# A feed-forward's convolution over tokens, done on transposed gates, is done instead on gates with tokens on the partitions

## The chip, the cores and the metric

The kernel runs on one core of a Trainium2 chip, which has eight. The metric is the time of one execution on the device, in microseconds (us). TensorE multiplies matrices, VectorE (DVE) and ScalarE (ACT) work on elements, GpSimd (POOL) does a small part, and SyncE (SP) and ScalarE issue the transfers, which run on the core's DMA engines. SBUF is the memory on the chip, with 128 partitions; PSUM takes TensorE's results.

## The reference

Two transformer blocks run one after the other on x of 256 tokens by 2048 channels, all in float32. The change touches the end of the second block, the feed-forward with a short causal convolution over the tokens on its gate:

```
h = rms_norm_2(x, ffn_norm_g[i])
val, gate = jnp.split(h @ w_up[i], 2, axis=-1)          # 2048 -> 2 x 5632
gate = causal_depthwise_conv(gate, conv_w[i], conv_b[i])
x = x + (val * jax.nn.gelu(gate, approximate=False)) @ w_down[i]

def causal_depthwise_conv(x, w, b):                     # w: 3 x 5632
    xp = jnp.pad(x, ((0, 0), (2, 0), (0, 0)))
    y = b
    for k in range(3):
        y = y + w[k] * xp[:, k:k + l]
    return y
```

Token s of a gate channel thus needs tokens s-1 and s-2 of the same channel. The first block's feed-forward has SiLU in place of convolution and GELU: silu(h @ w_gate) * (h @ w_up), then the down projection.

## The kernel before

**Panels and pieces.** Every matrix product is cut into panels of 512 output columns. The tokens are two tiles of 128 (t = 0, 1), so a panel has two accumulators in PSUM (`ACC`, four banks in all, two panels in turn). The rows of a weight panel come in chunks of 4 x 128 rows, one transfer of 1 MB each, in four slots; a chunk is two pieces. A piece of the wide panels is 2 x 128 rows of weights, and costs TensorE 12 products: for each tile and each 128 rows `weights_hi*xT_hi`, `weights_lo*xT_hi`, `weights_hi*xT_lo` (lines 602 to 604 in `panel`). A wide panel has 8 pieces.

**The split.** Float32 weights are cut in two before use. For each piece ScalarE writes the high part (`weights_hi`, line 1233) and VectorE the rest (`weights_lo`, line 1811). Both do it three pieces ahead of TensorE, in a ring of four: ScalarE's split of piece g+3 waits until TensorE has finished piece g-1, and TensorE waits for `lo_split` of a piece before its first product.

**Side work.** Everything else hangs in generators. After each piece every engine's program calls `side.step()`, which runs its next stretch of side work up to a `yield`; so a number of yields places side work in a panel. The engines' programs are written apart and meet by semaphores only. The order on each engine is thus fixed, and one that waits in a side step holds up its own next split.

**The second feed-forward** has 11 pairs of panels, gate then value ("up"). ScalarE evacuates the gate's accumulators to `ffn_gate` (`FF1`, line 1385) when the gate panel is multiplied, VectorE the value's to `ffn_hidden` (`FF2`, line 1971). Both have tokens on the partitions. `ffn_turn` then runs in the next gate panel's steps: TensorE transposes gates and values (line 626, product with an identity), 16 blocks of 128 x 128 for a pair, all after the second piece. With channels on the partitions the convolution is a shift along the row: VectorE computes it from PSUM (`conv2`, lines 2009 and 2015; its weights are one number for each partition), ScalarE does GELU (line 1404), VectorE multiplies with the value (line 2027), and the product is split into `hiddenT_hi` (ScalarE, line 1406) and `hiddenT_lo` (VectorE, line 2031), in two halves `kp`. After the last pair the turning has no spread: it comes after the first piece of the down projection.

**The first feed-forward** evacuates with SiLU (line 1385), multiplies in the evacuation of the value (line 1974), and so turns only products: 8 transposes for each pair, then one copy and one subtraction for each half (lines 1409 and 1992).

The convolution's weights come at the start as rows (`vectors`), are turned by TensorE, and lie in `V2`.

Of the kernel before, what the change touches and what calls it, by code (L numbers as in the profile page):

```python
# [14 lines left out]
P = 128  # L15
# [28 lines left out]
PIECES = 4  # L44
PAIRS = 8
# [45 lines left out]
class Events:  # L91
# [8 lines left out]
        mixed ffn_turned hidden_hi hidden_lo convolved gelu_ready gated_ready rows_applied  # L100
# [8 lines left out]
    LOADS = """x_load0 x_load1 x_load2 x_load3 x_load4 second_piece fourth_piece rows0 rows1 rows2 rows3 rows4 decay gla_b norm_rows dt b_proj c_proj v_bias sinks  # L109
        gate_rows0 gate_rows1 glu_rows stores""".split()  # L110
# [11 lines left out]
class Memory:  # L122
# [10 lines left out]
    def on_chip(self):  # L133
# [20 lines left out]
        self.V2 = small("vectors2", [P, 4 * KF])  # L154
# [55 lines left out]
        self.CG = sb("conv_gelu", [P, 2, S], R + 96 * K)  # L210
# [55 lines left out]
        self.ROWS = [sb(f"rows{i}", [P, P], 90 * K + R + 512 * i) for i in range(5)]  # L266
# [226 lines left out]
class Tensor:  # L493
# [8 lines left out]
    def program(self):  # L502
# [50 lines left out]
        self.ffn(plan.ffn1, side, False)  # L553
# [29 lines left out]
        self.ffn(plan.ffn2, side, True)  # L583
# [125 lines left out]
    def ffn(self, panels, side, second):  # L709
        m = self.m  # L710
        X = (m.XH, m.XL)
        for i, (gate, up) in enumerate(panels):
            if i:
                side.add(self.ffn_turn(panels[i - 1], second, spread=True))
# [3 lines left out]
        side.add(self.ffn_turn(panels[-1], second, spread=False))  # L718

    def ffn_turn(self, pair, second, spread):  # L720
# [3 lines left out]
        for kp in range(2):  # L724
# [399 lines left out]
class Scalar:  # L1124
# [161 lines left out]
    def load_rows4(self):  # L1286
        act, t, rows, ev = self.act, self.t, self.m.ROWS[4], self.ev
        vec = lambda x: x.rearrange("(k p) -> k p", p=P)
        at = 0
        for n in ("norm2_w", "attn_norm_g_2", "ffn_norm_g_2"):  # L1290
            act.dma_start(rows[at:at + KD, :], vec(t[n][0])).then_inc(ev["loaded_rows4"], 16)
            at += KD
        act.dma_start(rows[at:at + 2, :], vec(t["gla_norm_w"][0])).then_inc(ev["loaded_rows4"], 16)
        act.dma_start(rows[at + 2:at + 26, :],
                      t["conv_w"][0].rearrange("j (k p) -> (j k) p", p=P)).then_inc(ev["loaded_rows4"], 16)
# [6 lines left out]
    def vectors(self):  # L1302
        act, t, m, ev = self.act, self.t, self.m, self.ev
        vec = lambda x: x.rearrange("(k p) -> k p", p=P)
        cw = t["conv_w_2"][0].rearrange("j (k p) -> (j k) p", p=P)
        for i, at, n, src in ((1, 0, 88, cw[0:88, :]), (2, 0, 44, cw[88:132, :]), (2, 44, 44, vec(t["conv_b_2"][0])),
                              (3, 0, 14, vec(t["b_in_2"][0, 0:QKVU2])), (3, 14, 4, vec(t["ssm_d_2"][0])),
# [1173 lines left out]
```

## Time and profile before

| | |
|---|---|
| time, median of 3 runs | 2893.9 us (2893.78 to 2893.98) |
| the profiled execution's own time | 2893.83 us |
| its span in the profile | 2892.6 us |
| TensorE busy | 2879.3 us (100%) |
| VectorE / ScalarE busy | 1634.0 us (56%) / 1321.1 us (46%) |
| granted TensorE clock | 1.00 of full speed, 2.4 GHz, nearly throughout |

The busy share is that of the span. Matmuls overlap, so the busy time of TensorE shows that it seldom stood without work, and not how fast it went; the distance between the starts of two instructions shows what one of them costs.

### The profile page before, as it was taken

What the parts mean: (1) busy time and instruction counts of PE and PEld (TensorE: products, weight loads), DVE (VectorE), ACT (ScalarE), POOL (GpSimd) and SP (SyncE); (2) the same over time, 40 slices, a digit from 0 to 9 for tenths busy, and PEclk for the clock granted to TensorE, in tenths of its full rate; (3) what the DMA queues carried; (4) which work ended last, traced back from release to release, by engine and by line L of the source; (5) the groups of instructions that cost most, each with busy time, mean ns of one, the idle gap of its engine ahead of it and who ended that gap; (6) DMA issues with size and microseconds to landing.
All of it is one profiled execution on the core that took longest, in us unless ns stands there. A gap on an engine that the chain in (4) does not pass through costs nothing.

```text
span 2892.6 us, 32563 instructions
## 1 busy us (share of the span) xinstructions
PE 2879.3 (100%) x13522; PEld 2380.4 (82%) x13522; DVE 1634.0 (56%) x1874; ACT 1321.1 (46%) x1627; POOL 183.1 (6%) x221
## 2 busy tenths in 40 slices
PE   9999999999999999999999999999999999999998
PEld 8878887788888888888888888887888888888887
DVE  5464555555555554554475457655755665656444
ACT  5444445444444444444454455444554444444443
POOL 0000000000000000000000029900100000000000
PEclk9999999999999999999999999999999999999999
DMA  7555454555555555555665556554655555555563
GB/s 257 198 166 195 155 188 149 174 190 189 196 187 184 188 190 190 189 190 189 205 193 182 185 175 198 171 171 153 206 187 189 189 178 189 183 192 192 186 204 131
DMA packets 279392, 536.86 MB, mean 186 GB/s; under 512 B 17361, under 2 KB 20365, under 8 KB 279245
## 3 DMA queue, kind: packets, MB, share of 16 engines
q1 hardware_dynamic: 267520, 528.52, 55.8%
q10 hardware_dynamic: 11725, 6.27, 0.8%
q8 instruction: 107, 1.75, 0.2%
q14 instruction: 40, 0.33, 0.0%
HBM read 532.65 MB, written 2.10 MB: 185 GB/s over the span
## 4 chain that ended last, share of the span: by engine, by line
PE 99%; DVE 0%; ACT 0%; issue 0%; POOL 0%; POOLq 0%; ACTq 0%
PE panels L602 31%; PE panels L604 31%; PE panels L603 31%; PE side L626 3%; DVE weights_lo L1811 0%; PE side L919 0%; PE side L615 0%; PE side L996 0%; PE side L915 0%; PE side L904 0%; PE side L783 0%; PE side L1089 0%; PE side L1088 0%; PE side L1065 0%; PE side L800 0%; PE side L817 0%
## 5 line engine op out<-in xcount | busy, mean ns | idle before, releaser
L1811 DVE TENSOR_TENSOR weights_lo<-weights,weights_hi 128x1024 fp32r<-128x1024 f32 (+1 forms) x1032 | 1254.6, 1220 | 1077.5 <-ACT weights_hi L1233 1074.8
L1233 ACT ACTIVATE weights_hi<-weights 128x1024 fp32r<-128x1024 f32 (+1 forms) x1032 | 1066.3, 1036 | 1218.0 <-PE panels L604 1198.4
L602 PE MATMUL panels<-weights_hi,xT_hi 128*128 128x512 f32 (+1 forms) x2748 | 1077.4, 392 | 0.1
L604 PE MATMUL panels<-weights_hi,xT_lo 128*128 128x512 f32 (+1 forms) x2752 | 1069.3, 389 | 0.0
L603 PE MATMUL panels<-weights_lo,xT_hi 128*128 128x512 f32 (+1 forms) x2752 | 1068.7, 388 | 0.0
L602 PEld LDWEIGHTS panels<-weights_hi,xT_hi 128*128 128x128 f32 x2748 | 516.4, 188 | 111.1 <-issue 7.3
L604 PEld LDWEIGHTS panels<-weights_hi,xT_lo 128*128 128x128 f32 x2752 | 517.0, 188 | 107.3
L603 PEld LDWEIGHTS panels<-weights_lo,xT_hi 128*128 128x128 f32 x2752 | 517.5, 188 | 103.2 <-issue 0.2
L602 PE MATMUL panels<-weights_hi,hiddenT_hi 128*128 128x512 f32 x704 | 275.2, 391 | 0.0
L604 PE MATMUL panels<-weights_hi,hiddenT_lo 128*128 128x512 f32 x704 | 274.2, 390 | 0.0
L603 PE MATMUL panels<-weights_lo,hiddenT_hi 128*128 128x512 f32 x704 | 274.2, 389 | 0.0
L604 PEld LDWEIGHTS panels<-weights_hi,hiddenT_lo 128*128 128x128 f32 x704 | 132.2, 188 | 27.5
L602 PEld LDWEIGHTS panels<-weights_hi,hiddenT_hi 128*128 128x128 f32 x704 | 132.2, 188 | 27.2
L603 PEld LDWEIGHTS panels<-weights_lo,hiddenT_hi 128*128 128x128 f32 x704 | 132.3, 188 | 26.9
L402 POOL TENSOR_TENSOR rstd<-mean_squares,minus_half 128x2 f32<-128x2 f32 x5 | 4.4, 876 | 1270.4 <-DVE mean_squares L1874 1270.4
L602 PE MATMUL panels<-weights_hi,merged2T_hi 128*128 128x512 f32 x128 | 50.4, 394 | 0.3 <-issue 0.3
L602 PE MATMUL panels<-weights_hi,mixedT_hi 128*128 128x512 f32 x128 | 50.2, 392 | 0.0
L604 PE MATMUL panels<-weights_hi,merged2T_lo 128*128 128x512 f32 x128 | 49.9, 390 | 0.0
L604 PE MATMUL panels<-weights_hi,mixedT_lo 128*128 128x512 f32 x128 | 49.9, 390 | 0.0
L603 PE MATMUL panels<-weights_lo,merged2T_hi 128*128 128x512 f32 x128 | 49.9, 390 | 0.0
L603 PE MATMUL panels<-weights_lo,mixedT_hi 128*128 128x512 f32 x128 | 49.8, 389 | 0.0
L402 POOL TENSOR_TENSOR rstd_first<-mean_squares,minus_half 128x2 f32<-128x2 f32 x1 | 0.7, 688 | 737.9 <-DVE mean_squares L1874 737.9
(356 smaller groups left out, 1914.6 us busy)
## 6 DMA issues: line engine op xcount, KB each, us to landing
weights<-in_w_in SPq DMA_DIRECT2D x162, 1024.0 KB, 5.0
weights<-in_w_up SPq DMA_DIRECT2D x88, 1024.0 KB, 5.1
weights<-in_w_ffn_gate SPq DMA_DIRECT2D x44, 1024.0 KB, 5.2
weights<-in_w_ffn_up SPq DMA_DIRECT2D x44, 1024.0 KB, 5.2
weights<-in_w_out SPq DMA_DIRECT2D x32, 1024.0 KB, 5.1
weights<-in_w_ffn_down SPq DMA_DIRECT2D x32, 1024.0 KB, 5.1
weights<-in_w_down SPq DMA_DIRECT2D x32, 1024.0 KB, 5.1
weights<-in_w_ffn_down SPq DMA_DIRECT2D x16, 768.0 KB, 4.5
```

The source lines that it names most:

```text
L402: self.pool.tensor_tensor(dst[:, 0:2], self.m.MS[:, 0:2], self.m.NHALF[:, 0:2], ALU.pow).then_inc(self.ev["rstd_ready"])
L602: pe.matmul(acc, a, wh, start=k0 + k == 0, stop=False)
L603: pe.matmul(acc, a, wl, start=False, stop=False)
L604: inst = pe.matmul(acc, b, wh, start=False, stop=k0 + k == total - 1)
L626: return self.pe.transpose(out, in_, self.m.IDENT[0:in_.shape[0], 0:in_.shape[0]])
L1233: self.act.activation(self.m.HI[:, g % PIECES, 0:n], raw, ACT.Copy).then_inc(self.ev["hi_split"])
L1811: self.dve.tensor_tensor(m.LO[:, ring, 0:n], raw, m.HI[:, ring, 0:n].bitcast(F32), ALU.subtract).then_inc(self.ev["lo_split"])
```

## The change

The second feed-forward's convolution moves to where the gates have tokens on their partitions. The shift by one or two tokens is then a shift of partitions, and DMA makes it: after ScalarE has evacuated a gate panel, it issues six transfers from `ffn_gate` to two new tiles `gate_shifted1` and `gate_shifted2` (`shift_gates`): for each shift one of 112 partitions, one of 15 or 14, and one of 1 or 2 that takes the end of tile 0 to the start of tile 1. The weights and the bias are now needed as rows that are the same in all partitions: four transfers of 256 KB for each pair (`conv_rows`), issued by ScalarE behind the pair's GELU for the next pair.

VectorE's convolution (`conv2`) is six operations of 128 x 1024, two after each other for each shift, in steps 5 to 8 of the value panel; ScalarE's GELU is one operation of 128 x 1024 in its step 8. The value's evacuation multiplies by it at once, as in the first feed-forward, but waits for `gelu_ready`. TensorE then turns only the product, so both feed-forwards share `ffn_turn`. The convolution's weights no longer pass through `vectors`: three transfers, two transposes and two copies there are gone, and so is `V2`.

```diff
--- before.py
+++ after.py
...
-        self.CG = sb("conv_gelu", [P, 2, S], R + 96 * K)
+        self.GS1 = sb("gate_shifted1", [P, TT, PANEL], R + 96 * K)
+        self.GS2 = sb("gate_shifted2", [P, TT, PANEL], 80 * K + 512)
+        self.WR1 = sb("conv_rows01", [P, 2, PANEL], R + 40 * K)
+        self.WR2 = sb("conv_rows2b", [P, 2, PANEL], R + 84 * K)
...
-        for i, n, loads in ((1, 88, 1), (2, 88, 2), (3, 50, 4), (4, 74, 5)):
+        for i, n, loads in ((1, 50, 4), (2, 74, 5)):
...
-            if second:
-                b0, b1 = self.bank(2 * kp), self.bank(2 * kp + 1)
-                for k in range(2):
-                    for t in range(TT):
-                        f = (2 * kp + k) * P
-                        o = slice(k * S + t * P, k * S + (t + 1) * P)
-                        self.tr(b0[:, o], m.FF1[:, t, f:f + P])
-                        inst = self.tr(b1[:, o], m.FF2[:, t, f:f + P])
-                self.free(2 * kp, "gated_ready", n - 2 * (FF // PANEL))
-                self.free(2 * kp + 1, "gated_ready", n - 2 * (FF // PANEL))
-            else:
-                inst = self.four(self.bank(kp), lambda k, t: m.FF2[:, t, k * P:(k + 1) * P], 2 * kp)
-                self.free(kp, "hidden_lo", n)
-            inst.then_inc(ev["ffn_turned"])
-        for _ in range((5 if second else 4) if spread else (4 if second else 2)):
+            self.four(self.bank(kp), lambda k, t: m.FF2[:, t, k * P:(k + 1) * P], 2 * kp).then_inc(ev["ffn_turned"])
+            self.free(kp, "hidden_lo", n)
+        for _ in range(4 if spread else 2):
             yield
         if not spread:
-            for _ in range(5 if second else 0):
-                yield
             pe.wait_ge(ev["hidden_lo"], self.ffn_turns)
...
+        if second:
+            side.add(self.conv_rows(panels[0][0], self.plan.out2[-1].end))
...
-            if i and second:
-                act.wait_ge(ev["ffn_turned"], n0 + 2 * i)
...
+            if second:
+                side.finish()
+                self.shift_gates(gate)
+                side.add(self.gelu(i, panels))
             self.panel(up, side)
             side.finish()
-        side.add(self.ffn_turn(len(panels) - 1, second, spread=False, rows=rows, pair=panels[-1]))
-
-    def ffn_turn(self, i, second, spread, rows=None, pair=None):
+        side.add(self.ffn_turn(len(panels) - 1, spread=False, rows=rows, pair=panels[-1]))
+
+    def conv_rows(self, gate, end):
+        act, m, ev, t = self.act, self.m, self.ev, self.t
+        act.wait_ge(ev["multiplied"], end)
+        cols = slice(gate.col - FF, gate.col - FF + PANEL)
+        for dst, src in ((m.WR1[:, 0, :], t["conv_w_2"][0][0, cols]), (m.WR1[:, 1, :], t["conv_w_2"][0][1, cols]),
+                         (m.WR2[:, 0, :], t["conv_w_2"][0][2, cols]), (m.WR2[:, 1, :], t["conv_b_2"][0][cols])):
+            act.dma_start(dst, src.partition_broadcast(P)).then_inc(ev["loaded_conv_rows"], 16)
+        yield
+
+    def shift_gates(self, gate):
+        act, m, ev = self.act, self.m, self.ev
+        self.wait_evacuated(gate)
+        for s, dst in ((1, m.GS1), (2, m.GS2)):
+            act.dma_start(dst[s:MAIN + s, :, :], m.FF1[0:MAIN, :, :]).then_inc(ev["loaded_shifted"], 16)
+            act.dma_start(dst[MAIN + s:P, :, :], m.FF1[MAIN:P - s, :, :]).then_inc(ev["loaded_shifted"], 16)
+            act.dma_start(dst[0:s, 1, :], m.FF1[P - s:P, 0, :]).then_inc(ev["loaded_shifted"], 16)
+
+    def gelu(self, i, panels):
+        act, m, ev = self.act, self.m, self.ev
+        for _ in range(7):
+            yield
+        act.wait_ge(ev["convolved"], i + 1)
+        act.activation(m.FF1[:, :, :], m.FF1[:, :, :], ACT.Gelu).then_inc(ev["gelu_ready"])
+        if i + 1 < len(panels):
+            yield from self.conv_rows(panels[i + 1][0], panels[i][0].end)
...
-            if second:
-                yield
-                k = n - 2 * (FF // PANEL)
-                act.wait_ge(ev["convolved"], k)
-                act.activation(m.CG[:, :, :], m.CG[:, :, :], ACT.Gelu).then_inc(ev["gelu_ready"])
-                act.wait_ge(ev["gated_ready"], k)
-                act.activation(hh, m.CG[:, :, :], ACT.Copy).then_inc(ev["hidden_hi"])
-            else:
-                act.wait_ge(ev["ffn_turned"], n)
-                act.activation(hh, m.SIDE[:, kp, :], ACT.Copy).then_inc(ev["hidden_hi"])
+            act.wait_ge(ev["ffn_turned"], n)
+            act.activation(hh, m.SIDE[:, kp, :], ACT.Copy).then_inc(ev["hidden_hi"])
             yield
             if spread and kp == 0:
                 yield
-                if not second:
-                    yield
+                yield
...
+        if second:
+            dve.memset(m.GS1[0:1, 0, :], 0.0)
+            dve.memset(m.GS2[0:2, 0, :], 0.0)
         for i, (gate, up) in enumerate(panels):
             if i:
-                side.add(self.ffn_turn(i - 1, second, spread=True))
+                side.add(self.ffn_turn(i - 1, spread=True))
             self.panel(gate, side)
+            if second:
+                side.finish()
+                side.add(self.conv2(i))
             self.panel(up, side)
             side.finish()
             dve.wait_ge(ev["multiplied"], up.end)
             if i:
                 dve.wait_ge(ev["ffn_turned"], n0 + 2 * i)
             for t in range(TT):
-                acc, r = m.ACC[:, (up.index % 2) * TT + t, :], m.RSTD[:, t:t + 1]
                 if second:
-                    dve.tensor_scalar(m.FF2[:, t, :], acc, r, None, ALU.mult).then_inc(up.evac[t][0])
+                    dve.wait_ge(ev["gelu_ready"], i + 1)
                 else:
                     dve.wait_ge(*gate.evac[t])
-                    dve.scalar_tensor_tensor(out=m.FF2[:, t, :], in0=acc, scalar=r, in1=m.FF1[:, t, :],
-                                             op0=ALU.mult, op1=ALU.mult).then_inc(up.evac[t][0])
-        side.add(self.ffn_turn(len(panels) - 1, second, spread=False))
-
-    def ffn_turn(self, i, second, spread):
+                dve.scalar_tensor_tensor(out=m.FF2[:, t, :], in0=m.ACC[:, (up.index % 2) * TT + t, :],
+                                         scalar=m.RSTD[:, t:t + 1], in1=m.FF1[:, t, :], op0=ALU.mult,
+                                         op1=ALU.mult).then_inc(up.evac[t][0])
+        side.add(self.ffn_turn(len(panels) - 1, spread=False))
...
+    def conv2(self, i):
+        dve, m, ev, step = self.dve, self.m, self.ev, self.step
+        w0, w1, w2, bias = (r[:, j, :].unsqueeze(1).to_broadcast([P, TT, PANEL]) for r in (m.WR1, m.WR2) for j in range(2))
+        g = m.FF1[:, :, :]
+        for _ in range(4):
+            yield
+        dve.wait_ge(ev["loaded_shifted"], 16 * 6 * (i + 1))
+        dve.wait_ge(ev["loaded_conv_rows"], 16 * 4 * (i + 1))
+        step(dve.tensor_tensor(g, g, w2, ALU.mult))
+        for shifted, w in ((m.GS1, w1), (m.GS2, w0)):
+            yield
+            step(dve.tensor_tensor(shifted[:, :, :], shifted[:, :, :], w, ALU.mult))
+            step(dve.tensor_tensor(g, g, shifted[:, :, :], ALU.add))
+        yield
+        dve.tensor_tensor(g, g, bias, ALU.add).then_inc(ev["convolved"])
+        yield
```

On TensorE this is the row of the second feed-forward where the first pair is turned, before and after (`side` is the PSUM tile that takes transposes).

```order
L603 MATMUL panels<-weights_lo,xT_hi 128x512
L604 MATMUL panels<-weights_hi,xT_lo 128x512
L626 MATMUL side<-identity,ffn_gate 128x128
L626 MATMUL side<-identity,ffn_hidden 128x128
L626 MATMUL side<-identity,ffn_gate 128x128
L626 MATMUL side<-identity,ffn_hidden 128x128
L626 MATMUL side<-identity,ffn_gate 128x128
L626 MATMUL side<-identity,ffn_hidden 128x128
```

```order
L606 MATMUL panels<-weights_lo,xT_hi 128x512
L607 MATMUL panels<-weights_hi,xT_lo 128x512
L629 MATMUL side<-identity,ffn_hidden 128x128 x8
L605 MATMUL panels<-weights_hi,xT_hi 128x512
L606 MATMUL panels<-weights_lo,xT_hi 128x512
L607 MATMUL panels<-weights_hi,xT_lo 128x512
L605 MATMUL panels<-weights_hi,xT_hi 128x512
```

Of the sixteen transposes for each pair, the eight of the gates are gone (the first block shows half of the sixteen); their place behind the second piece is the same.

On VectorE, from the evacuation of the first value panel on. Before:

```order
L2031 TENSOR_TENSOR hiddenT_lo<-conv_gelu,hiddenT_hi 128x512
L1811 TENSOR_TENSOR weights_lo<-weights,weights_hi 128x1024 x10
L1971 TENSOR_SCALAR ffn_hidden<-panels,rstd 128x512 x2
L1811 TENSOR_TENSOR weights_lo<-weights,weights_hi 128x1024 x2
L2009 TENSOR_SCALAR conv_gelu<-side,vectors_59 128x256 x2
L2015 SCALAR_TENSOR_TENSOR conv_gelu<-side,vectors_59,conv_gelu 128x255 x2
L2015 SCALAR_TENSOR_TENSOR conv_gelu<-side,vectors_59,conv_gelu 128x254 x2
L1811 TENSOR_TENSOR weights_lo<-weights,weights_hi 128x1024
L2027 TENSOR_TENSOR conv_gelu<-side,conv_gelu 128x512
L2031 TENSOR_TENSOR hiddenT_lo<-conv_gelu,hiddenT_hi 128x512
L1811 TENSOR_TENSOR weights_lo<-weights,weights_hi 128x1024 x2
L2009 TENSOR_SCALAR conv_gelu<-side,vectors_59 128x256 x2
```

After, from the last splits of the second value panel (`conv_rows01`, `conv_rows2b` are weights and bias, `gate_shifted1` and `2` the shifted gates; the number behind a name tells copies apart):

```order
L1817 TENSOR_TENSOR weights_lo<-weights,weights_hi 128x1024 x8
L2014 TENSOR_TENSOR ffn_gate<-ffn_gate,conv_rows2b 128x1024
L1817 TENSOR_TENSOR weights_lo<-weights,weights_hi 128x1024
L2017 TENSOR_TENSOR gate_shifted_108<-gate_shifted_108,conv_rows_110 128x1024
L2018 TENSOR_TENSOR ffn_gate<-ffn_gate,gate_shifted_108 128x1024
L1817 TENSOR_TENSOR weights_lo<-weights,weights_hi 128x1024
L2017 TENSOR_TENSOR gate_shifted_109<-gate_shifted_109,conv_rows_110 128x1024
L2018 TENSOR_TENSOR ffn_gate<-ffn_gate,gate_shifted_109 128x1024
L1817 TENSOR_TENSOR weights_lo<-weights,weights_hi 128x1024
L2020 TENSOR_TENSOR ffn_gate<-ffn_gate,conv_rows2b 128x1024
L1985 SCALAR_TENSOR_TENSOR ffn_hidden<-panels,rstd,ffn_gate 128x512 x2
L1817 TENSOR_TENSOR weights_lo<-weights,weights_hi 128x1024 x2
```

The convolution went from the gate panel that follows, between two and three splits behind the evacuation, to the last four splits of the value panel itself, ahead of the evacuation.

On ScalarE, before, from the second gate panel's end, and after, the same place:

```order
L1385 ACTIVATE ffn_gate<-panels,rstd 128x512 x2
L1233 ACTIVATE weights_hi<-weights 128x1024 x11
L1404 ACTIVATE conv_gelu<-conv_gelu 128x512
L1406 ACTIVATE hiddenT_hi<-conv_gelu 128x512
L1233 ACTIVATE weights_hi<-weights 128x1024 x3
L1404 ACTIVATE conv_gelu<-conv_gelu 128x512
L1406 ACTIVATE hiddenT_hi<-conv_gelu 128x512
L1233 ACTIVATE weights_hi<-weights 128x1024 x2
```

```order
L1370 ACTIVATE ffn_gate<-panels,rstd 128x512 x2
L1393 DMA gate_shifted_108<-ffn_gate 112x1024
L1394 DMA gate_shifted_108<-ffn_gate 15x1024
L1395 DMA gate_shifted_108<-ffn_gate 1x16x32
L1393 DMA gate_shifted_109<-ffn_gate 112x1024
L1394 DMA gate_shifted_109<-ffn_gate 14x1024
L1395 DMA gate_shifted_109<-ffn_gate 2x512
L1222 ACTIVATE weights_hi<-weights 128x1024 x8
L1402 ACTIVATE ffn_gate<-ffn_gate 128x1024
L1386 DMA conv_rows_110<-in_conv_w 128x512 x2
L1386 DMA conv_rows2b<-in_conv_w 128x512
L1386 DMA conv_rows2b<-in_conv_b 128x512
```

The six shifting transfers stand ahead of the split that follows the evacuation; GELU and four more transfers stand ahead of the split of the next gate panel's fourth piece.

## Rows read from the trace of the kernel before

**Rows 1.** The page: span, busy time and share of each engine, times instructions.

```profile
span 2892.6 us, 32563 instructions
...
PE 2879.3 (100%) x13522; PEld 2380.4 (82%) x13522; DVE 1634.0 (56%) x1874; ACT 1321.1 (46%) x1627; POOL 183.1 (6%) x221
```

**Rows 2.** The page: the chain that ended last, shares by engine.

```profile
PE 99%; DVE 0%; ACT 0%; issue 0%; POOL 0%; POOLq 0%; ACTq 0%
```

**Rows 3.** ScalarE's timeline: gate evacuations of both feed-forwards (start, duration, instruction).

```profile
1008.55 1.27 ACT L1385 ACTIVATE ffn_gate<-panels,rstd 128x512 f32<-128x512 f32 x2 [1.60 <-PE panels L604]
...
1052.99 1.27 ACT L1385 ACTIVATE ffn_gate<-panels,rstd 128x512 f32<-128x512 f32 x2 [1.60 <-PE panels L604]
...
2166.03 1.27 ACT L1385 ACTIVATE ffn_gate<-panels,rstd 128x512 f32<-128x512 f32 x2 [1.60 <-PE panels L604]
...
2211.34 1.27 ACT L1385 ACTIVATE ffn_gate<-panels,rstd 128x512 f32<-128x512 f32 x2 [1.54 <-PE panels L604]
```

**Rows 4.** TensorE's timeline, a block of sixteen transposes, second feed-forward.

```profile
2192.80 0.40 PE L604 MATMUL panels<-weights_hi,xT_lo 128*128 128x512 f32 x1
2193.03 0.27 PE L626 MATMUL side<-identity,ffn_gate 128*128 128x128 f32 x1
2193.14 0.27 PE L626 MATMUL side<-identity,ffn_hidden 128*128 128x128 f32 x1
...
2195.01 0.39 PE L603 MATMUL panels<-weights_lo,xT_hi 128*128 128x512 f32 x1
```

**Rows 5.** TensorE's weight loads, the same place.

```profile
2192.80 0.14 PEld L626 LDWEIGHTS side<-identity,ffn_gate 128*128 128x128 f32 x1
```

**Rows 6.** TensorE's timeline, the four vector transposes near the start.

```profile
47.38 0.72 PE L626 MATMUL side<-identity,rows 88*128 88x88 f32 x4
...
48.22 0.39 PE L603 MATMUL panels<-weights_lo,xT_hi 128*128 128x512 f32 x1
```

**Rows 7.** VectorE's timeline in the second feed-forward.

```profile
2187.78 1.41 DVE L1971 TENSOR_SCALAR ffn_hidden<-panels,rstd 128x512 f32<-128x512 f32 x2 [0.34 <-PE panels L604]
...
2194.11 1.00 DVE L2009 TENSOR_SCALAR conv_gelu<-side,vectors 128x256 f32<-128x256 f32 x2 [1.23 <-PE side L626]
2195.14 1.78 DVE L2015 SCALAR_TENSOR_TENSOR conv_gelu<-side,vectors,conv_gelu 128x255 f32<-128x255 f32 x4
2196.83 1.22 DVE L1811 TENSOR_TENSOR weights_lo<-weights,weights_hi 128x1024 fp32r<-128x1024 f32 x1
...
2223.32 1.23 DVE L1811 TENSOR_TENSOR weights_lo<-weights,weights_hi 128x1024 fp32r<-128x1024 f32 x1 [1.43 <-ACT weights_hi L1233]
2226.10 1.23 DVE L1811 TENSOR_TENSOR weights_lo<-weights,weights_hi 128x1024 fp32r<-128x1024 f32 x1 [1.55 <-ACT weights_hi L1233]
```

**Rows 8.** ScalarE by line and shape, 2140 to 2650 us: count, busy, mean.

```profile
L1233 ACT ACTIVATE weights_hi<-weights 128x1024 fp32r<-128x1024 f32 x180 | 189.5, 1058 | 199.5 <-PE panels L604 197.2 <-POOL rstd L402 2.3
...
L1404 ACT ACTIVATE conv_gelu<-conv_gelu 128x512 f32<-128x512 f32 x21 | 13.3, 633 | 40.3 <-DVE conv_gelu L2015 40.3
```

**Rows 9.** Tile gate_bias_rows: issue duration (min/median/max ns) and microseconds to landing.

```profile
L1685 ACTq DMA_DIRECT2D gate_bias_rows<-in_b_in x8: 334/334/353, 1761.2 to 1939.2; - x8
...
DMA to landing us min/median/max: 3.0/4.7/6.3
```

**Rows 10.** Tile rows: the longest issue on ScalarE's queue.

```profile
L1291 ACTq DMA_DIRECT2D rows<-in_norm_w x1: 607/607/607, 37.7 to 37.7; - x1
```

**Rows 11.** Transfers: size of each, median microseconds to landing.

```profile
weights<-in_w_up SPq DMA_DIRECT2D x88, 1024.0 KB, 5.1
...
norm_rows<-in_final_norm_g ACTq DMA_DIRECT2D x1, 1024.0 KB, 4.9
...
w_a_down<-in_w_in ACTq DMA_DIRECT2D x1, 128.0 KB, 17.1
```

**Rows 12.** Busy time of each engine by stretch, at the end, with granted clock (PEclk).

```profile
core 0: us, PE busy (x) PEld busy (x) DVE busy (x) ACT busy (x) POOL busy (x), PEclk, DMA share, GB/s
...
2880.00:2884.00 4.00, 1.94 (x9) 1.28 (x7) 2.63 (x4) 1.32 (x4) 0.00 (x0) 1.00 0.00 0
2884.00:2888.00 4.00, 0.00 (x0) 0.00 (x0) 2.31 (x7) 1.89 (x4) 0.69 (x1) 0.63 0.33 125
```

More of the change, by code:

```diff
@@ L265, in on_chip @@
         self.FF2 = sb("ffn_hidden", [P, TT, PANEL], R + 92 * K)
-        self.ROWS = [sb(f"rows{i}", [P, P], 90 * K + R + 512 * i) for i in range(5)]
+        self.ROWS = [sb(f"rows{i}", [P, P], 90 * K + R + 512 * i) for i in range(3)]
 class Plan:
@@ L552, in program @@
         self.residual(plan.out1, (m.MH, m.ML), side, rows=False, turn=True)
-        self.ffn(plan.ffn1, side, False)
+        self.ffn(plan.ffn1, side)
         side.add(self.ssm_setup())
@@ L707, in residual, with ffn @@
             side.add(self.norm_panel(p, pan, rows, turn))
-    def ffn(self, panels, side, second):
+    def ffn(self, panels, side):
         m = self.m
@@ L713, in ffn @@
             if i:
-                side.add(self.ffn_turn(panels[i - 1], second, spread=True))
+                side.add(self.ffn_turn(panels[i - 1], spread=True))
             self.panel(gate, X, side)
@@ L717, in ffn, with ffn_turn @@
             side.finish()
-        side.add(self.ffn_turn(panels[-1], second, spread=False))
-    def ffn_turn(self, pair, second, spread):
+        side.add(self.ffn_turn(panels[-1], spread=False))
+    def ffn_turn(self, pair, spread):
         pe, ev, m = self.pe, self.ev, self.m
@@ L1284, in turn, with load_rows2 @@
             yield
-    def load_rows4(self):
-        act, t, rows, ev = self.act, self.t, self.m.ROWS[4], self.ev
+    def load_rows2(self):
+        act, t, rows, ev = self.act, self.t, self.m.ROWS[2], self.ev
         vec = lambda x: x.rearrange("(k p) -> k p", p=P)
@@ L1867, in vectors @@
             yield
-        for i in (1, 2, 3, 4):
+        for i in (1, 2):
             self.dve.wait_ge(self.ev["vectors"], i + 1)
@@ L1958, in ffn @@
         n0 = 2 * len(panels) if second else 0
+        if second:
+            dve.memset(m.GS1[0:1, 0, :], 0.0)
+            dve.memset(m.GS2[0:2, 0, :], 0.0)
         for i, (gate, up) in enumerate(panels):
             if i:
-                side.add(self.ffn_turn(i - 1, second, spread=True))
+                side.add(self.ffn_turn(i - 1, spread=True))
             self.panel(gate, side)
+            if second:
+                side.finish()
+                side.add(self.conv2(i))
             self.panel(up, side)
@@ L1984, in ffn_turn @@
             self.ffn_turns += 1
[L1985 to L1993 removed]
+            k = slice(at + 2 * kp, at + 2 * kp + 2)
+            self.dve.wait_ge(self.ev["hidden_hi"], self.ffn_turns)
+            self.dve.tensor_tensor(m.HL[:, k, :], m.SIDE[:, kp, :], m.HH[:, k, :].bitcast(F32),
+                                   ALU.subtract).then_inc(self.ev["hidden_lo"])
             yield
@@ L1996, in ffn_turn @@
                 yield
-                if not second:
-                    yield
-    def conv2(self, at, kp):
-        dve, m, ev, n = self.dve, self.m, self.ev, self.ffn_turns
-        G, b0 = m.CG, m.SIDE[:, 2 * kp, :]
-        vec = lambda j, k: m.V2[:, at + (j * KF + 2 * kp + k):at + (j * KF + 2 * kp + k) + 1]
-        dve.wait_ge(ev["ffn_turned"], n)
-        if n > 1:
-            dve.wait_ge(ev["hidden_hi"], n - 1)
-            dve.wait_ge(ev["hidden_lo"], n - 1)
-        for k in range(2):
-            self.mark(dve.tensor_scalar(G[:, k, :], b0[:, k * S:(k + 1) * S], vec(2, k), vec(3, k),
-                                        ALU.mult, ALU.add))
-        for j in (1, 0):
-            s = 2 - j
-            self.settle()
-            for k in range(2):
-                inst = dve.scalar_tensor_tensor(
-                    out=G[:, k, s:S], in0=b0[:, k * S:(k + 1) * S - s], scalar=vec(j, k), in1=G[:, k, s:S],
-                    op0=ALU.mult, op1=ALU.add)
-                if j:
-                    self.mark(inst)
-        inst.then_inc(ev["convolved"])
```

53 lines of the change are left out of this document (16 added, 37 removed).

## Prediction

> **What bounds the kernel now.** I read the page first: TensorE is busy for 2879.3 of the span's 2892.6 us [rows 1], and 99% of the chain that ended last are its instructions [rows 2]. So there is hardly a wait to remove. An edit pays if it takes instructions from TensorE's row, and costs where TensorE must wait for something new. What VectorE and ScalarE do is free until TensorE waits for it. Next I read ScalarE's evacuations of the gates, which mark the pairs: the pairs of the first feed-forward lie 1052.99 - 1008.55 = 44.44 us apart, those of the second 2211.34 - 2166.03 = 45.31 us [rows 3]. Both have the same 192 products; they differ by 8 transposes. The other pairs repeat these distances within 0.03 us.
>
> **What TensorE saves.** The difference, 45.31 - 44.44 = 0.87 us, is the price of the 8 gate transposes of a pair, 0.109 us each. The block itself agrees: from the product at 2192.80 to the one at 2195.01 are 2.21 us, of which two product distances of 0.227 (44.44 us less 0.87 for the first feed-forward's own 8 transposes, by 192) are no transposes, so (2.21 - 0.45) / 16 = 0.110 [rows 4]. Eleven pairs: 11 x 0.87 = **-9.6 us**. Near the start four vector transposes take 48.22 - 47.38 - 0.23 = 0.61 us [rows 6]; two of them go: **-0.3 us**. The transfers and copies that go with them lie on ScalarE beside a busy TensorE: nothing.
>
> **What ScalarE gets.** I count from the start of a gate's evacuation, 2211.34 [rows 3], as zero. A piece lasts 2.72 us: the value panel's eight end at 2187.78 - 2166.03 = 21.75 [rows 3, 7]. The evacuation ends at 1.27. It is awaited (hand-overs take 0.03: VectorE's two operations from 2194.11 end at 2195.11, the dependent one starts at 2195.14 [rows 7]), and then come six transfers to issue. The trace shows no issue of a copy from SBUF to SBUF. The nearest row is 0.334 us each for 128 rows [rows 9], the longest 0.607 [rows 10]: together 2.0 to 3.6. Then the split, 1.06 [rows 8], and VectorE's, 1.23 [rows 7]: done at 5.7 to 7.3. Behind the waiting split stands TensorE's fourth piece. Its weight load would start at 3 x 2.72 less 0.42 = 7.74, since a load stands about 0.42 ahead of the moment at which the others see the piece before as done (2192.80 [rows 5] against 2187.78 + 5.44 [rows 7]). It is in time at both ends: nothing. The four broadcast transfers behind GELU are 1.3 us of issue by 0.334 and precede a split that TensorE wants at 21.75 + 7.74 = 29.5; ScalarE is free for it by 27. Nothing.
>
> **Do the shifts land in time?** The first multiplication comes at 13.1 (below). The issues end by 1.3 + 3.6 = 4.9 at the latest, which leaves 8.2 us. Both shifts are 896 KB. The rows for transfers from HBM beside the same weight stream: 256 KB 3.0 to 6.3 us [rows 9], 1 MB 4.9 us, a weight chunk 5.1 [rows 11]. I take 5 to 6.5: in time. The other end is 17.1 us for a transfer of short runs in the crowded start [rows 11]. I keep it for a rival, as these runs are long. The weight chunks themselves are issued some 19 us (seven pieces) before their first split and need 5.1, so they have room for 2 MB more for each pair.
>
> **When VectorE lets the products go.** This is the step that decides. The convolution stands in the value panel's steps 5 to 8, each behind a split. The split of step 5 starts at 2223.32 - 2211.34 = 11.98, that of step 6 at 2226.10 - 2211.34 = 14.76 [rows 7]. Back to back the next operation starts 0.09 before the one ahead ends (the run from 2195.14 ends at 2196.92, the next starts at 2196.83 [rows 7]), so a split of 1.23 costs 1.14. The six operations of 128 x 1024 have the shape of the split; I take its 1.22, and 1.25 where the next must wait for the result. First multiplication: 13.12 to 14.34, before the next split. Then from 14.76 without a pause: split 1.14, two operations 2.50, split 1.14, two operations 2.50, split 1.14, bias 1.22. Convolved at 24.40. GELU on ScalarE: 128 x 1024 takes 1.06 in the split; GELU at 512 costs 0.633, of which a second 512 would add about the same 0.43 [rows 8]. 24.43 + 1.06 = 25.49. The evacuation with the product: two operations, 1.41 [rows 7], so 25.52 + 1.41 = 26.93, and TensorE sees it at 26.96.
>
> TensorE wants it after two pieces of the next gate panel: the first transpose's load started at 2192.80, 5.02 behind the panel's end [rows 5, 7], that is at 21.75 + 5.02 = 26.77. It is late by 0.19. Of this, 0.12 costs nothing, because a transpose's product normally starts 0.23 behind its load (2193.03 [rows 4, 5]) and needs only the 0.11 of a transpose's distance. That leaves 0.07; I take 0.1, for ten pairs **+1.0 us**.
>
> The eleventh pair has no such room: it is turned after one piece of the down projection, so wanted at 26.77 - 2.72 = 24.05. Late by 2.91, less 0.12: **+2.8 us**. Before, the value was free at 21.75 + 1.41 and nothing waited. Nothing else is late next: while TensorE stands, both splits catch up, and `hidden_lo` of this pair follows in time: from the transposes at 27.2, ScalarE has two copies of 0.63 and two splits of 1.06 [rows 8], to 30.6, then VectorE's subtraction of some 0.7, to 31.3. TensorE wants it after two more pieces, at 33.
>
> Bounds. If the six operations were as slow as two evacuations of 512 (1.41), the five behind 14.76 would add 0.95: 1.0 a pair more, and 2899. If they took only ScalarE's 1.06, nothing waits in the ten pairs and the last waits 2.0: 2886.0.
>
> **Sum.** -9.6 - 0.3 + 1.0 + 2.8 = -6.1 us against the profiled execution's own 2893.83: 2887.7. The median of the runs is 0.07 above it, so 2887.8 us. A measurement of this kernel tells about 0.2% (5.8 us) from no change; the line is at 2888.1, so the forecast lies on it.
>
> **A rule and a row.** TensorE's last work ends 1.94 us behind 2880, at 2881.94. The granted clock is 1.00 (2.4 GHz) over 2880 to 2884 and averages 0.63 over 2884 to 2888 [rows 12]; if it fell in one step to half (1.2 GHz), then at about 2885.0, 3.1 us after the last work. The wait at the last pair is 2.8 us. The Trainium skill, "TensorE: Matmul & The Clock Gate", section "Part 1: The HAM clock gate", says that activity holds the clock up and an idle TensorE falls to half rate; the trace agrees with the fall. By the rule the stall may cost more than its length; by the sum it costs its length alone.
>
> **The rivals.**
> *No wait in the ten pairs.* Speaks for it that 0.07 is less than the error of a sum of ten durations. Then 2886.8. Chance 0.12.
> *A larger wait.* A broadcast operand, or a longer hand-over than 0.03 at each of five places, puts 0.3 to 1.0 on each pair: 2890 to 2898. Against it: no row shows a 1024 operation in SBUF slower than 1.22 here, while GpSimd is idle. Chance 0.18.
> *The clock falls at the last pair.* For it the rows above, against it that 2.8 is under what passed there. Each us at half speed costs 0.5 more; for 2 to 8 us, 2889 to 2892. Chance 0.07.
> *The shifts land late* (the other side). Each us beyond 13.1 delays the whole chain by one in all eleven pairs. It decides from 1.1 us late on: 6.1 + 5.8 = 11.9 us by 11. With the 17.1 of [rows 11] for the last transfer: 4.9 + 17.1 - 13.1 = 8.9 late, 98 us, near 2986. Against it are all rows of long transfers. Chance 0.08.
> *The gates still pass TensorE*: excluded by the order of rows above.
> The forecast itself, waits of 0 to 0.2 a pair, 2886.8 to 2889, has 0.5, two thirds of it below the line; 0.05 is for what I don't see.
>
> **How the numbers follow.** Faster: 0.33 + 0.12 = 0.45. Slower: 0.08 and half of what I don't see, 0.11. The rest, 0.44, is within 0.2%. The range leaves out the upper part of the larger wait and the late landing, and reaches below to all operations at 1.06: 2886.0 to 2895.0.
>
> **What would show it.** Right: pairs of the second feed-forward 44.44 to 44.6 apart; GELU starting 24.4 behind the gate's evacuation; eight transposes of products only; a wait of 2.8 us of TensorE ahead of the last transposes, for the value's evacuation. Wrong: VectorE's first multiplication idle for a DMA; splits waited for by TensorE; pairs above 45; a clock under 1.00 near 2640.

## The result and the profile after

The changed kernel takes 2898.52 us (median; 2896.94 to 2899.77 in 20 runs), the kernel before in the same comparison 2893.82 us (2893.35 to 2894.09). The ratio is 1.0016, 95% interval 1.001 to 1.0023: 4.7 us slower, where 2887.8 was forecast and 2895.0 was the end of the range. By the bound of 0.2% that is no change, but the interval leaves out equality, and the forecast gain of 6 us is not there. The runs also spread over 2.8 us, against 0.7 before.

The page of the changed kernel's profiled run (2898.11 us) shows where to look. These are its span, TensorE's part of the busy line, the queue that carries the shifts, and the chain.

```profile
span 2896.8 us, 32398 instructions
PE 2875.9 (99%) x13432; PEld 2367.3 (82%) x13432; DVE 1634.1 (56%) x1788; ACT 1313.8 (45%) x1614; POOL 183.6 (6%) x221
q10 hardware_dynamic: 21702, 29.18, 3.3%
PE 95%; ACTq 2%; DVE 1%; ACT 1%; issue 0%; DMA 0%; SPq 0%; POOL 0%; DVEq 0%
```

Against [rows 1] TensorE has 90 instructions and 3.4 us of busy time less (99% of the span where it was 100%). The span is 4.2 us longer. Against [rows 2] the chain has lost 4% to others, the largest of them ACTq: instructions that issue transfers on ScalarE. DMA has 0% of it (rounded), so hardly anything on the path waited for bytes. The waits between 2150 and 2700 us say who waits for whom (us in total, times, longest). In the kernel before none of TensorE's rows stands in this list.

```profile
ACT ffn_gate L1402 <- DVE ffn_gate L2020: 46.7, 11, 4.4
DVE ffn_hidden L1985 <- ACT ffn_gate L1402: 13.4, 11, 1.2
PEld side L629 <- issue: 9.5, 11, 3.3
PEld panels L605 <- DVE weights_lo L1817: 6.9, 11, 0.9
PE side L629 <- DVE ffn_hidden L1985: 5.1, 11, 2.9
PE panels L605 <- DVE weights_lo L1817: 2.1, 10, 0.5
```

Two waits have come, each eleven times. One is for VectorE's split of a weight piece (L1817), the other, ahead of the transposes (L629), for the evacuation with the product (L1985). A wait's length is not its cost: a weight load normally runs ahead of its product, so what is lost is read from the distances of the products.

**The first wait, on ScalarE.** ScalarE's timeline at the pair of [rows 3], with its issues (ACTq), up to the next pair:

```profile
2210.87 1.27 ACT L1370 ACTIVATE ffn_gate<-panels,rstd 128x512 f32<-128x512 f32 x2 [1.60 <-PE panels L607]
2212.22 0.59 ACTq L1393 DMA_DIRECT2D gate_shifted<-ffn_gate  x1
2212.85 0.86 ACTq L1394 DMA_DIRECT2D gate_shifted<-ffn_gate  x1
2213.74 0.87 ACTq L1395 DMA_DIRECT2D gate_shifted<-ffn_gate  x1
2214.64 0.61 ACTq L1393 DMA_DIRECT2D gate_shifted<-ffn_gate  x1
2215.28 0.81 ACTq L1394 DMA_DIRECT2D gate_shifted<-ffn_gate  x1
2216.11 0.65 ACTq L1395 DMA_DIRECT2D gate_shifted<-ffn_gate  x1
2216.81 3.90 ACT L1222 ACTIVATE weights_hi<-weights 128x1024 fp32r<-128x1024 f32 x4 [4.67 <-PE panels L607]
...
2235.88 1.06 ACT L1402 ACTIVATE ffn_gate<-ffn_gate 128x1024 f32<-128x1024 f32 x1 [4.37 <-DVE ffn_gate L2020]
...
2256.20 1.27 ACT L1370 ACTIVATE ffn_gate<-panels,rstd 128x512 f32<-128x512 f32 x2 [1.60 <-PE panels L607]
```

The six issues take 4.39 us of their own, 4.54 from the first's start to the last's end, where the forecast allowed 2.0 to 3.6. The split behind them starts at 2216.81. The bracket names TensorE as its releaser, but that product had long been done (the idle time of 4.67 is filled by the issues). TensorE's timeline shows who pays:

```profile
2218.61 0.39 PE L607 MATMUL panels<-weights_hi,xT_lo 128*128 128x512 f32 x1
2219.18 0.50 PE L605 MATMUL panels<-weights_hi,xT_hi 128*128 128x512 f32 x1 [0.19 <-DVE weights_lo L1817]
2219.52 0.39 PE L606 MATMUL panels<-weights_lo,xT_hi 128*128 128x512 f32 x1
```

Three products start 0.57 and 0.34 us apart instead of 0.23 and 0.23: 0.45 us lost in each of the eleven pairs.

**The second wait, ahead of the transposes.** VectorE's timeline in the same pair, to be held against [rows 7]:

```profile
2217.91 4.63 DVE L1817 TENSOR_TENSOR weights_lo<-weights,weights_hi 128x1024 fp32r<-128x1024 f32 x4 [7.38 <-ACT weights_hi L1222]
...
2226.18 1.23 DVE L1817 TENSOR_TENSOR weights_lo<-weights,weights_hi 128x1024 fp32r<-128x1024 f32 x1 [0.49 <-ACT weights_hi L1222]
...
2234.63 1.22 DVE L2020 TENSOR_TENSOR ffn_gate<-ffn_gate,conv_rows2b 128x1024 f32<-128x1024 f32 x1
2237.07 1.41 DVE L1985 SCALAR_TENSOR_TENSOR ffn_hidden<-panels,rstd,ffn_gate 128x512 f32<-128x512 f32 x2 [1.22 <-ACT ffn_gate L1402]
```

From the split at 2226.18 to the end of the bias at 2235.85 are 9.67 us; the forecast had 24.40 - 14.76 = 9.64. All six operations last 1.22 to 1.23: the broadcast operands cost nothing. Then the hand-overs: GELU ends at 2236.94 and VectorE goes on at 2237.07, and the product ends at 2238.48. TensorE's timeline goes on:

```profile
2238.13 0.39 PE L607 MATMUL panels<-weights_hi,xT_lo 128*128 128x512 f32 x1
2238.74 1.06 PE L629 MATMUL side<-identity,ffn_hidden 128*128 128x128 f32 x8 [0.22 <-DVE ffn_hidden L1985]
2239.56 0.48 PE L605 MATMUL panels<-weights_hi,xT_hi 128*128 128x512 f32 x1
2239.88 0.39 PE L606 MATMUL panels<-weights_lo,xT_hi 128*128 128x512 f32 x1
```

and in its weight loads the first transpose stands at

```profile
2238.71 0.86 PEld L629 LDWEIGHTS side<-identity,ffn_hidden 128*128 128x128 f32 x8 [0.61 <-issue]
```

Without a wait the products around eight transposes would stand 0.227 + 0.87 = 1.10 us apart, and the next 0.23. They stand 1.43 and 0.32 apart: 0.42 lost per pair, 0.1 forecast.

**The last pair.** TensorE's timeline once more, and the stretches around it with the granted clock:

```profile
2643.61 0.39 PE L607 MATMUL panels<-weights_hi,hiddenT_lo 128*128 128x512 f32 x1
2646.94 1.94 PE L629 MATMUL side<-identity,ffn_hidden 128*128 128x128 f32 x8 [2.94 <-DVE ffn_hidden L1985]
2648.53 0.77 PE L605 MATMUL panels<-weights_hi,hiddenT_hi 128*128 128x512 f32 x1
2649.10 0.63 PE L606 MATMUL panels<-weights_lo,hiddenT_hi 128*128 128x512 f32 x1
2649.53 0.60 PE L607 MATMUL panels<-weights_hi,hiddenT_lo 128*128 128x512 f32 x1
2649.95 0.41 PE L605 MATMUL panels<-weights_hi,hiddenT_hi 128*128 128x512 f32 x1
```

```profile
core 0: us, PE busy (x) PEld busy (x) DVE busy (x) ACT busy (x) POOL busy (x), PEclk, DMA share, GB/s
2640.00:2643.00 3.00, 3.00 (x15) 2.49 (x14) 2.93 (x4) 0.00 (x0) 0.00 (x0) 1.00 0.87 264
...
2645.00:2647.00 2.00, 0.06 (x1) 0.09 (x2) 1.73 (x3) 1.09 (x2) 0.00 (x0) 0.89 0.00 0
2647.00:2649.00 2.00, 2.00 (x9) 2.00 (x10) 1.12 (x2) 0.94 (x2) 0.00 (x0) 0.50 0.01 3
2649.00:2651.00 2.00, 2.00 (x8) 1.54 (x8) 1.75 (x3) 1.09 (x2) 0.00 (x0) 0.76 0.91 287
```

For 3.3 us TensorE started neither a product nor a load; between the end of one product (2644.00) and the start of the next it stood 2.94. The granted clock was 1.00 up to 2646.50 and 0.50, which is 1.2 GHz, from 2646.75 on: it fell some 0.3 us before the wait ended, 2.6 us after the last work. The eight transposes then take 1.94 us instead of 1.06, and the next four products start 0.57, 0.43 and 0.42 apart. To the product at 2650.44, the sixth behind the transposes, 4.6 us are lost. Of these 3.14 are the wait (the load stands 3.30 behind 2643.61, where in the ten pairs 0.58 stand for a loss of 0.42) and the other 1.5 are work at the half clock.

**Where the time went,** as spans. The first gate of the second feed-forward is evacuated at 2165.57, 0.46 earlier than before. Eleven minus one pairs take 453.51 us (2165.57 to 2619.08) against 453.03: 8.7 saved, 10 x 0.45 and 10 x 0.42 lost, 0.5 left over as small change. Half of this is one pair (2346.83 to 2392.42, 45.59 us): there the fourth issue starts 0.35 behind the third's end instead of 0.03, and the split behind the issues comes later by 0.26. From there to the end 277.72 against 273.54: 0.87 saved, 0.45 and 4.6 lost. Together +4.2 us.

### The profile page after: what moved, and what is told of

Its sections match the earlier page's. It is cut to its first block, busy times and chain, and to the rows that moved or that the text cites. A ratio compares the mean times of both kernels' runs of the same rounds, so it can differ in the third digit from the quotient of the medians.

```text
span 2896.8 us, 32398 instructions
## 1 busy us (share of the span) xinstructions
PE 2875.9 (99%) x13432; PEld 2367.3 (82%) x13432; DVE 1634.1 (56%) x1788; ACT 1313.8 (45%) x1614; POOL 183.6 (6%) x221
## 4 chain that ended last, share of the span: by engine, by line
PE 95%; ACTq 2%; DVE 1%; ACT 1%; issue 0%; DMA 0%; SPq 0%; POOL 0%; DVEq 0%
PE panels L605 30%; PE panels L607 30%; PE panels L606 30%; PE side L629 2%; DVE weights_lo L1817 1%; ACTq L1394 1%; ACTq L1395 1%; ACT ffn_gate L1370 0%; ACT weights_hi L1222 0%; ACTq L1393 0%; DMA x<-in_x 0%; PE side L908 0%; PE side L985 0%; PE side L904 0%; PE side L893 0%
## 5 line engine op out<-in xcount | busy, mean ns | idle before, releaser
L1817 DVE TENSOR_TENSOR weights_lo<-weights,weights_hi 128x1024 fp32r<-128x1024 f32 (+1 forms) x1032 | 1249.6, 1218 | 1102.1 <-ACT weights_hi L1222 1098.8
```

The costliest lines, as they stand in the source:

```text
L1817: self.dve.tensor_tensor(m.LO[:, ring, 0:n], raw, m.HI[:, ring, 0:n].bitcast(F32), ALU.subtract).then_inc(self.ev["lo_split"])
```

## The experiments

Seven kernels in two batches. The kernel before took 2893.68 us beside the first four and 2893.80 us beside the other three. Each is held against the changed kernel's 2898.5; the ratio is to the kernel before.

**1. One split ahead of the shifts' issues.** Nothing is taken away; the six issues come one split later on ScalarE.

```diff
-    def panel(self, pan, side, dense=False):
+    def panel(self, pan, side, dense=False, done=0):
         for g in range(pan.first, pan.end):
-            self.split(g + AHEAD)
+            if g >= pan.first + done:
+                self.split(g + AHEAD)
...
             if second:
                 side.finish()
+                self.split(up.first + AHEAD)
                 self.shift_gates(gate)
...
-            self.panel(up, side)
+            self.panel(up, side, done=1 if second else 0)
```

> ScalarE does the split of the value panel's fourth piece ahead of the six shifting transfers; all else as in the changed kernel (2898.5). Theory of three waits (the six issues hold up the split, 0.45 a pair; the product comes late for the transposes, 0.42 a pair; the last pair waits and loses the clock, 4.6 once): the first goes, 11 x 0.45 = 5.0, and 0.1 a pair of the second with it: 2892.5, pairs 44.8 apart, no wait of TensorE for a split. Rival, traffic (23 MB more on the same DMA engines slow the loads or TensorE itself): the same bytes run, so 2898.5. Rival, the shifts land too late for the convolution: later by 1.1 a pair, 2905 or more.

Measured: 2892.24 us (2891.08 to 2893.29), ratio 0.9994 [0.9985 to 1.0003]. TensorE's waits for the splits are gone from the list and the other wait stays. This row answers to `PE side L629` of the changed kernel:

```profile
PE side L629 <- DVE ffn_hidden L1987: 5.2, 11, 2.9
```

The pairs lie 44.84 us apart (2210.28 to 2255.12; 45.33 in the changed kernel). So the queue of issues in front of the split, and not the loss of ScalarE's time as such, was the cost: 0.49 a pair by these distances, 11 x 0.45 of it the wait itself, the rest small change that goes with it.

The clock blurs the comparison a little. In this kernel's own profile it stayed at 1.00 through the last wait, which is as long as before; in the changed kernel's it fell. The mean granted clock of the single runs tells them apart: it is 0.998 in 18 of the changed kernel's 20 runs (2897.9 to 2899.8 us) and 0.999 in two (2896.9 and 2897.0); here it is 0.998 in six (2892.2 to 2893.3) and 0.999 in five (2891.1 to 2891.4). Runs with the same clock differ by 5.8 to 6.0 us between the two kernels, the two groups of one kernel by 1.3 to 1.5.

**2. The convolution one step earlier on VectorE.**

```diff
-        for _ in range(4):
+        for _ in range(3):
             yield
```

> VectorE's convolution starts one piece earlier (steps 4 to 7 of the value panel); all else as in the changed kernel. Theory of three waits: the product is ready about 24.5 behind the gate's evacuation instead of 27.6, so no pair waits at the transposes (4.2 less) and the last waits about 0.5 and keeps the clock (4 less): 2890.3; the wait for the split, 0.45 a pair, stays. Traffic rival: 2898.5. Rival, the shifts land only just in time now: VectorE's first multiplication waits for a DMA and the gain is smaller by that.

Measured: 2890.60 us (2889.68 to 2891.24), ratio 0.9989 [0.998 to 0.9998]. The waits of the ten pairs ahead of the transposes are gone. What is left, and the wait for the splits that this edit doesn't touch:

```profile
PEld panels L605 <- DVE weights_lo L1817: 6.6, 11, 0.9
...
PE side L629 <- DVE ffn_hidden L1985: 0.5, 1, 0.5
```

The two waits are thus independent, and an earlier start of the convolution, at the same length, removes the second. VectorE has no wait for the shifts in this kernel's list, so they had landed a piece earlier too.

**3. The last pair turned one piece later,** on all three engines.

```diff
-        if spread:
+        if spread or pair is self.plan.ffn2[-1]:
             yield
...
```

> Only the eleventh pair is changed: its transposes come after the second piece of the down projection instead of the first, on all three engines. Theory of three waits: its wait shrinks from 3.3 to that of the other pairs, the granted clock stays 1.00 near 2645 us, and 4.6 - 0.4 = 4.2 go: 2894.3. If the fall of the clock were not due to the wait, only 2.7 go: 2895.8. Traffic rival: 2898.5. If the varying clock makes the spread of the times (2896.9 to 2899.8, before 2893.4 to 2894.1), it shrinks to below 1 us here and stays in e1.

Measured: 2894.41 us (2893.95 to 2894.92), ratio 1.0003 [0.9994 to 1.0011], 4.1 us from one wait. Its wait ahead of the transposes is now as short as the others, and the clock at the place is whole:

```profile
PE side L629 <- DVE ffn_hidden L1985: 2.4, 11, 0.2
```

```profile
2645.00:2647.00 2.00, 1.77 (x10) 1.23 (x9) 1.97 (x3) 1.80 (x2) 0.00 (x0) 1.00 0.00 0
2647.00:2649.00 2.00, 2.00 (x15) 1.74 (x13) 2.00 (x3) 1.63 (x3) 0.00 (x0) 1.00 0.25 14
```

The mean clock is 0.999 in all eleven runs, and their spread falls from 2.8 to 1.0 us: most of the changed kernel's spread came from this wait.

**4. All three edits,** the diffs above together.

> The three edits together: split ahead of the shifts, convolution one piece earlier, last turn one piece later. Theory of three waits: all of 5.0 + 4.2 + 4.6 go, which leaves the saved transposes: 2893.8 - 9.6 - 0.4 = 2883.8, pairs 44.44 apart, at most 0.3 more. Traffic rival: 2898.5, or a part of the way.

Measured: 2884.30 us (2883.74 to 2884.89), ratio 0.9967 [0.9955 to 0.998]. The pairs lie 44.41 us apart (2209.74 to 2254.15), nine of the ten distances within 44.41 and 44.45, which is the first feed-forward's distance [rows 3]: here the transposes' price of 0.87 is seen whole. The shifts and the weights' rows still move all their 2.0 MB a pair, so what the changed kernel lost was not the DMA traffic beside TensorE. The single edits gave 6.3, 7.9 and 4.1, together 18.3; the three at once give 14.2. The second edit also shortens the last wait (from 2.9 to 0.5 us), and the first gave 1.3 us more than its 11 x 0.45, in part by the clock there; most of both lies in what the third removes. What waits now is VectorE's first multiplication, for the shifts:

```profile
DVE ffn_gate L2016 <- DMA gate_shifted<-ffn_gate: 17.0, 11, 2.7
...
PE side L629 <- DVE ffn_hidden L1987: 0.2, 1, 0.2
```

It costs next to nothing yet. TensorE's only wait left stands in the pair with the longest of these waits (2.7 us): that pair is the remaining distance, 44.81 us, 0.4 longer than the others.

**5. The shifts in transfers of 127 and 126 partitions,** as one would write them first; two wraps remain, four transfers in all.

```diff
-            act.dma_start(dst[s:MAIN + s, :, :], m.FF1[0:MAIN, :, :]).then_inc(ev["loaded_shifted"], 16)
-            act.dma_start(dst[MAIN + s:P, :, :], m.FF1[MAIN:P - s, :, :]).then_inc(ev["loaded_shifted"], 16)
+            act.dma_start(dst[s:P, :, :], m.FF1[0:P - s, :, :]).then_inc(ev["loaded_shifted"], 16)
...
```

> The changed kernel with one transfer of 127 (and one of 126) partitions in place of each pair of 112 and 15 (or 14): four issues a pair instead of six, the same bytes. Theory (the Trainium skill, 'DMA: Bandwidth & Descriptors', section 'Why a DMA increments its semaphore by 16 and not by 1': a transfer runs on the largest number of engines up to 16 that divides its row count, so 127 rows run on one, and 126 on 14): 127 rows of 4 KB on one DMA engine, at the 0.1 us that a 2 KB packet of the weights takes there on average, are about 25 us, so VectorE's first multiplication waits some 15 us a pair and the whole is about 11 x 15 slower than the changed kernel: 3050 to 3100. Rival, issue cost alone: two issues fewer (1.7 us) let the split come in time, 0.45 a pair less: 2893.5.

Measured: 3114.39 us (3110.12 to 3115.96), ratio 1.0761 [1.0744 to 1.0777], above the expected 3100: 19.6 us on each pair. The stretch in which only the first shift moves, and ScalarE's timeline there:

```profile
2235.00:2240.00 5.00, 1.97 (x9) 1.31 (x7) 0.00 (x0) 0.00 (x0) 0.00 (x0) 1.00 0.06 26
```

```profile
2230.52 0.66 ACTq L1393 DMA_DIRECT2D gate_shifted<-ffn_gate  x1
2231.22 8.76 ACTq L1394 DMA_DIRECT2D gate_shifted<-ffn_gate  x1
```

A share of 0.06 of sixteen DMA engines is one engine, and it moves 26 GB/s. In the changed kernel the 112-partition shifts moved at 229 to 311 GB/s (the quarters of a us that its two shifts fill, between 2213.5 and 2217.75). The Trainium skill, "DMA: Bandwidth & Descriptors", section "Why a DMA increments its semaphore by 16 and not by 1", says that the number of engines is the largest up to 16 that divides the partitions of both sides, one for 127; the trace agrees. What I had not expected is the second row: the issue of the small wrap, which otherwise takes 0.7 us, lasted 8.76 behind the slow transfer (median 4.8 over the 22), and held ScalarE's splits with it. TensorE then waits twice in a pair for a split, up to 7.1 us, and once ahead of the transposes, up to 6.7; VectorE waits up to 11.0 us for the bytes. The clock falls in these waits: behind the one that ends at 2243.94 products start 0.43 us apart instead of 0.23, and from 2165 to 2880 its mean is 0.87 to 0.89. The expected time left out both the blocked issue and the clock; this experiment doesn't tell their parts.

**6. The six issues on SyncE** instead of ScalarE, behind the last weight chunk that needn't wait for the split of the value panel's fourth piece (chunk `gate.end // 2 + SLOTS`).

```diff
+            for gate, up in self.plan.ffn2:
+                if c == gate.end // 2 + SLOTS:
+                    self.shift_gates(gate)
...
+    def shift_gates(self, gate):
+        sp, m, ev = self.sp, self.m, self.ev
+        for t in range(TT):
+            sp.wait_ge(*gate.evac[t])
...
-                self.shift_gates(gate)
...
```

> The six shifting transfers are issued from SyncE's queue, behind the weight chunk after which it has time, instead of from ScalarE's; all else as in the changed kernel (2898.5). Theory (their issue on ScalarE holds up the split): the wait for the split goes, as in the run with the split first: 2892.3, with ScalarE's split of the value panel's fourth piece right behind the evacuation. Rival, the transfers themselves take something from the split or from TensorE: no better than 2896. Rival, they now hold up the weight loads on SyncE's queue: ScalarE's splits wait for weights, above 2898.5.

Measured: 2892.60 us (2891.05 to 2894.42), ratio 0.9997 [0.9988 to 1.0005]. The issues are about as long on SyncE (count, min/median/max in ns):

```profile
L374 SPq DMA_DIRECT2D gate_shifted<-ffn_gate x22: 561/588/622, 2167.1 to 2617.7; - x22
L375 SPq DMA_DIRECT2D gate_shifted<-ffn_gate x22: 807/828/1466, 2167.7 to 2618.4; - x22
L376 SPq DMA_DIRECT2D gate_shifted<-ffn_gate x22: 567/641/897, 2168.7 to 2619.2; - x22
```

The waits for splits are gone as in the first experiment, and the weight chunks queued behind come in time. So the length goes with the transfer and not with the engine that issues it. The last pair's wait is as in the changed kernel, 2.9 us, and the clock falls there (0.998 in nine of the eleven runs).

**7. The diff of experiment 6 with those of 2 and 3.**

> As the run before, with the convolution one piece earlier and the last turn one piece later as in the run of all three edits (2884.3). ScalarE is free of the six issues. Theory: TensorE has nothing left to wait for in either, so the same 2884.3 within 0.5; it would be slower only if weight loads behind the shifts come late.

Measured: 2884.13 us (2883.90 to 2884.28), ratio 0.9967 [0.9954 to 0.9979], spread 0.4 us. TensorE waits for nothing in the whole second feed-forward. It can't be told from the fourth in time. Both are faster than the kernel before by 9.5 us and than the changed one by 14.

## Why the prediction was wrong

**What bounds the kernel: right.** An instruction less on TensorE is worth its distance as long as nothing new is waited for.

**What TensorE saves: right, 9.6 us.** Experiments 4 and 7 show the pairs at 44.41 to 44.45. Almost without waits they gain 10.0 and 10.1 us on the kernel before in the spans of the profiles (9.4 and 9.7 in the medians of the runs), which is this term and the start, where 0.3 was forecast and the first gate comes 0.5 to 0.7 earlier.

**"What ScalarE gets": the step that failed.** Its two ends for six issues, 2.0 and 3.6 us, came from the nearest row and the longest row of other transfers. Both ends were called in time, and the upper had only 0.5 us to spare against 7.74. Measured are 4.54 from first to last. VectorE takes over from ScalarE's split at 2217.91 - 2210.87 = 7.04 and is done 1.23 later, at 8.27, 0.53 behind 7.74: a loss of 0.45, eleven times, 5.0 us of the 10.3 by which the span missed. A bound taken from rows is only a bound if the rows are of the same thing. The question to ask was from where on it would cost: by the forecast's own terms at 7.74 - 1.30 - 1.06 - 1.23, about 4.1 us of issues, only 0.5 beyond the end of the range. Experiments 1 and 6 show this cost on its own.

**"When VectorE lets the products go": right in its mechanism, too small in two terms.** The operations were as long as forecast. Off were the hand-overs, taken as 0.03 from one row within VectorE. Between engines they are 0.13 (ScalarE to VectorE) and 0.23 (VectorE to TensorE's load), 0.3 more together. The chain also starts 15.31 behind the gate's evacuation instead of 14.76, 0.1 more than the 0.45 by which TensorE itself is late there. Together 0.5 with the 0.07 forecast; a product stood 0.03 behind its load, not 0.11, which gives 0.08 back, and 0.42 is measured. For the ten pairs 3.2 us more. The rival of a larger wait named this mechanism (0.3 to 1.0 a pair) and had 0.18; that its 2890 to 2898 all but reach the measured time is luck, since half of the miss is the wait for the splits, which no rival named. Experiment 2 shows the wait on its own.

**The last pair: 2.8 forecast, 4.6 measured.** 0.3 is the same hand-overs. The other 1.5 is the half clock, the rival with 0.07. I set it low because the wait was shorter than the 3.1 us that passed between last work and fall at the end [rows 12]. That one row was no bound either: here TensorE stood only 2.94 us, and the clock fell 2.6 us after the last work. Experiment 3 shows 4.1 us for the place. The Trainium skill, "TensorE: Matmul & The Clock Gate", section "Part 1: The HAM clock gate", says that an idle TensorE falls to half rate; the trace agrees, but the profiled run of experiment 1 kept the clock through the same wait, as did two of the changed kernel's 20 runs by their mean clock. Here its price differs from run to run, 0 or about 1.5 us.

**The transfers: right.** They landed in time. In the changed kernel the DMA engines move nothing between 2218.0 and 2220.0, so the shifts' bytes had passed by 2218.0, 1.2 us behind the last issue's end, 6.5 ahead of the first multiplication: no weight chunk was under way beside the shifts. In experiment 4 the earlier split frees a slot, a weight chunk is issued at 2213.24 among the shifts, its bytes run ahead of those of the second shift, and VectorE goes on only at 2221.30, 5.6 us behind the last issue's end at 2215.66; 5 to 6.5 was taken. The rival of the late landing, as large as it was put, came true in no run but the fifth.

The terms together: 5.0 + 3.2 + 1.8 + 0.5 of small change in the pairs, less 0.15 at the start, are 10.3, the distance between the -6.1 forecast and the +4.2 us measured in the spans. What makes the half of the small change that is not the one slow issue, and what decides whether the clock falls, stays open.

## What to carry to other kernels

When work goes to the DMA engines, price its issues on the engine that gives them, each shape apart, and look at what that engine owes the bound engine right behind them: here six issues of 0.6 to 0.9 us in front of one 1 us split undid half of the saving, and moving them behind that split cost nothing. When two ends of a bound give the same answer, work out from where on the answer changes; if that lies near one of the ends, it is not settled. Where an operation's result crosses engines, take hand-overs from rows that cross the same engines, and split a transfer whose partitions divide badly.

## What the hardware showed beyond that

- An issue of a copy within SBUF costs 0.60 us for 112 partitions, but 0.84 for 15 or 14 and 0.72 for 1 or 2 (medians): the small remainders are the dearer ones. Broadcasts from HBM to 128 partitions cost 0.33 [rows 9], and 0.33 to 0.47 for the convolution's rows.
- An issue took 8.76 us behind a transfer that went on one DMA engine (experiment 5), where it takes 0.7 otherwise.
- The wait that lets the clock fall makes the runs spread. Kernels without it spread by 0.4 to 1.2 us (experiments 3, 4 and 7) or 1.6 (experiment 2, where 0.5 us of it is left), those with it by 2.2 to 3.4 (the changed kernel, 1 and 6).
